# One key projection moved in quarters into the last steps of attention C

## The reference

```python
proj = u @ w_in[l]
qa, ka, va, qb, kb, vb, qc, kc, vc, gl = jnp.split(proj, split_at, axis=-1)
oa = neighbourhood_attention(...)                       # attention A, 8 heads of 64
ob = sliding_window_attention(apply_rope(qb), apply_rope(kb), vb, sw_sink[l])   # B, 8 q heads, 2 k/v heads
oc = differential_attention(apply_rope(qc), apply_rope(kc), vc, ...)            # C, 4 double heads
# inside C: a = softmax(q1 k1) - lam * softmax(q2 k2); o = a @ v; rmsnorm(o, subln_g) over the 128 values of a head
yb = branches @ w_branch[l];  merged = sum(sigmoid(gl + b_gate) * yb);  h = h + rmsnorm(merged @ w_out[l])
```

## Time and profile before

| what | us |
|---|---|
| median of 3 runs | 3376.05 (3374.82 to 3377.39) |
| the profiled execution, its own time | 3378.53 |
| its span, from the first to the last instruction | 3376.7 |
| PE busy | 3318.4 (98% of the span) |
| DVE busy | 2444.0 (72%) |
| ACT busy | 1688.9 (50%) |
| POOL busy | 845.7 (25%) |

### The profile page before, as it was taken

The page is one execution under the profiler, slowest core; times in us unless marked ns, Lnnn a source line. Parts: engine busy times, 40 slices in busy tenths (PEclk is TensorE's granted clock), DMA queues, the critical chain, the costliest instruction groups (busy, mean ns, idle before and its releaser), DMA issues. The chain is left out here.

```text
span 3376.7 us, 51734 instructions
## 1 busy us (share of the span) xinstructions
PE 3318.4 (98%) x20422; PEld 2953.5 (87%) x20422; DVE 2444.0 (72%) x3936; ACT 1688.9 (50%) x3071; POOL 845.7 (25%) x607
## 2 busy tenths in 40 slices
PE   9999999999999999999999999999999999999998
PEld 7999887878889998999887888889988888888998
DVE  7878765756697779777766656697768676649776
ACT  5545453635454445445454544454546374335543
POOL 3433111021054414432111021063400001206431
PEclk9999999999999999999999999999999999999999
DMA  4333433262223332333433253233332222322332
GB/s 138 106 99 114 112 94 86 68 144 91 88 94 104 102 108 75 106 106 114 110 84 94 70 151 99 69 100 103 105 97 92 88 83 69 105 91 92 98 109 82
DMA packets 118049, 332.79 MB, mean 99 GB/s; under 512 B 18984, under 2 KB 21800, under 8 KB 117808
## 3 DMA queue, kind: packets, MB, share of 16 engines
q1 hardware_dynamic: 105200, 306.30, 28.9%
q0 software_dynamic: 12320, 22.66, 3.3%
q10 hardware_dynamic: 288, 0.52, 0.1%
HBM read 306.23 MB, written 4.21 MB: 92 GB/s over the span
## 5 line engine op out<-in xcount | busy, mean ns | idle before, releaser
L1906 DVE TENSOR_TENSOR wl<-raw,wh 128x1024 fp32r<-128x1024 f32 (+2 forms) x633 | 801.2, 1270 | 276.8 <-ACT wh L1328 270.5
L1328 ACT ACTIVATE wh<-raw 128x1024 fp32r<-128x1024 f32 (+2 forms) x637 | 553.5, 875 | 385.1 <-PE PS L807 367.3
L807 PE MATMUL PS<-bh,wh 128*128 128x256 f32 x2520 | 708.5, 281 | 14.6 <-ACT tmp L1328 8.6
L807 PE MATMUL PS<-bl,wh 128*128 128x256 f32 x2520 | 702.7, 279 | 0.0
L807 PE MATMUL PS<-bh,wl 128*128 128x256 f32 x2520 | 702.7, 279 | 0.0
L807 PE MATMUL PS<-uh,wh 128*128 128x512 f32 (+2 forms) x1656 | 615.5, 372 | 13.5 <-DVE ul L1942 6.7
L807 PE MATMUL PS<-uh,wl 128*128 128x512 f32 (+2 forms) x1656 | 602.7, 364 | 0.0
L807 PE MATMUL PS<-ul,wh 128*128 128x512 f32 (+2 forms) x1656 | 602.3, 364 | 0.0
L807 PEld LDWEIGHTS PS<-bh,wh 128*128 128x128 f32 x2520 | 472.9, 188 | 23.1 <-DVE wl L1906 10.8
L807 PEld LDWEIGHTS PS<-bl,wh 128*128 128x128 f32 x2520 | 473.4, 188 | 0.0
L807 PEld LDWEIGHTS PS<-bh,wl 128*128 128x128 f32 x2520 | 471.9, 187 | 0.4
(11 more groups left out here) (268 smaller groups left out, 5748.6 us busy)
## 6 DMA issues: line engine op xcount, KB each, us to landing
raw<-in_gu SPq DMA_DIRECT2D x218, 512.0 KB, 3.3
raw<-in_win SPq DMA_DIRECT2D x139, 512.0 KB, 3.3
raw<-in_dn SPq DMA_DIRECT2D x80, 320.0 KB, 2.9
raw<-in_dn SPq DMA_DIRECT2D x40, 512.0 KB, 3.6
raw<-in_wbr SPq DMA_DIRECT2D x72, 256.0 KB, 2.7
raw<-in_wout SPq DMA_DIRECT2D x24, 512.0 KB, 3.2
raw<-in_dn SPq DMA_DIRECT2D x40, 256.0 KB, 2.6
raw<-in_wv SPq DMA_DIRECT2D x20, 512.0 KB, 3.2
```

Source lines behind the costliest of these rows:

```text
L807: return e.matmul(out, lhs, rhs, start=start, stop=stop, skip_group_check=True)
L1328: return e.activation(out, in_, f, scale=scale, **more)
L1906: tt(wl[:, c % 4, 0:n], src, wh[:, c % 4, 0:n], SUB).then_inc(*S.lo.up(("lo", c)))
```

## The change

The k projection of attention B is no longer a job of its own after attention C. `attention` makes its generator (`tail`) for attention C and takes one piece of six matmuls from it at steps n = 16, 17, 18 and 20. The piece stands ahead of what else the step does. The fourth piece, at n = 20, stands ahead of the sums of the last head. Only PE's program is touched.

```diff
@@ -1134,6 +1134,7 @@
                 A = ATT[st]
                 jobs = iter(fill.jobs)
                 now, left = iter(()), [0]
+                tail = dense(JOBS["k", v, "B", 0], v, "u") if st == "C" else iter(())
...
@@ -1164,6 +1165,8 @@
                             scores(v, st, n, b, qs[hh], *ks[hh], S.sc, (st, v, n))
                     if n < len(fill.quota):
                         filler(fill.quota[n])
+                    elif n in (A.n, A.n + 1, A.n + 2, A.n + 4):
+                        next(tail, None)
...
@@ -1248,7 +1251,6 @@
                 values(v, "C")
                 attention(v, "C", FILLS[v, "C"])
-                run(JOBS["k", v, "B", 0], v)
                 late = [JOBS["q", v, "B", 0], JOBS["t", v, "B"], JOBS["g", v, 1, 0], JOBS["g", v, 1, 1]]
```

## The result

The changed kernel took 3370.05 us (median of 13 runs, 3365.88 to 3374.96) where the kernel before took 3377.24 in the same comparison (13 runs, 3372.07 to 3383.62). The ratio of the times is 0.9982, with a 95% interval from 0.9974 to 0.9989. So by the ratio it is faster by about 6 us, between 3.7 and 8.8; the two medians are 7.2 apart. The forecast was 3369.0, a gain of 7.0.

What follows compares the result with a forecast made beforehand. PE, busy 98% of the span, was taken as the bound. Per mixer -2.75 (waits) - 1.72 (clock) + 0.97 (given back) = -3.50 us, -7.0 for two: 3376.05 - 7.0 = 3369.0 us, range 3364.3 to 3373.3.

Steps and rivals of the forecast that it cites:

- Term 1: Tail of attention C: the quarters of k cover PE's waits and their wake, -2.75 us per mixer.
- Term 2: k projection behind the tail: the granted clock no longer falls, -1.72 us per mixer.
- the clock still falls: Rival, behind the tail: only the waits go, nothing is given back, -5.5 us in all, 3370.5 us; chance 0.13.
- Term 3: Up to the branch products: DVE turns k only behind the diagonals, so +0.97 us per mixer is given back.
- The sum: Terms 1 to 3 together: -3.50 us per mixer, -7.0 for two, 3369.0 us by the median.
- The jam at attention A: Rival, start of attention A: small time shifts make a mixer 4.2 us cheaper or dearer, 3364.8 or 3373.2 us; chance 0.15.
- The slower rival: k's rotation lands late and stops PE at the branch products; at twice its time +3.7, 3379.7 us; chance 0.05.
- more is given back: Rival, tail: more given back or quarters wait; last sums 1.5 us later, gain 2.0 per mixer, 3372.0 us; chance 0.12.

Runs made afterwards that it cites:

- the useless quarter: Kernel before, plus six dense matmuls into k's bank, overwritten afterwards, ahead of the last head's sums: 3373.07 us, ratio 0.9992 [0.9983, 1.0001].

## Why the prediction was right

**Term 1, the waits, -2.75 us per mixer.** Right. The tail with k took 13.09 us where 13.05 was worked out: 10.36 + 5.44 - 13.09 = 2.71 us were gained. Seen from S, the 44.65 of before with the clock and the giveback taken away gives 44.65 - 1.61 - 40.35 = 2.69. All quarters covered their waits, also the fourth, whose margin was thin. That the sum is so near is luck in part: the four quarters took 1.48, 1.48, 1.46 and 1.48 us, 5.90 in all and not 5.44, and the short matmuls 13.09 - 5.90 = 7.19 and not 7.61. The two errors cancel. For the fourth quarter the longer time was of use: it started at 522.36, and the squares of head 3 were ready at 523.14 + 0.59 = 523.73, so that 1.36 us would have been just too short.

**Term 2, the clock, -1.72 us.** The size was right where the clock falls (1.61 by the useless quarter). The reason was only half right. I had taken the fall for an effect of ten light microseconds, and the quarters spread over them as its cure. The runs show that for the fall behind the last sums the last quarter decides: with the three others alone it fell in four of four tails, with the fourth alone in none of two. The one fall inside the tail shows that the last wait is not the only place for it, and why it comes at one place, at the other or not at all stays open. And the term was too large by the share of tails without a fall: over eight tails of before it is 7/8 of 1.6, 1.4 us. The prediction had one profile of before and took the fall, the same in both of its mixers, for fixed. The rival "the clock still falls" did not come true in any of the four tails of the changed kernel.

**Term 3, the giveback, +0.97 us.** Right in its mechanism, a little high: it measured 41.23 - 40.35 = 0.88, 0.56, 0.77 and 0.75 us in four tails. The spread is that of the landing of k's rotation, which now stands in the chain: 5.61, 5.29, 5.49 and 5.48 us from POOL's issue to DVE's release in the same tails. Its chain ran as written: the diagonals ended 528.56 - 523.84 = 4.72 us after the sums' start (4.77 foretold), the first diagonal product had no wait, and the wait for the low parts was 1.14 us where "about 1.2" was foretold. The turning of k ahead of the norms takes it away, which shows that the late turning is its cause.

**The sum.** Mean S over the profiles is 44.46 before and 41.09 now, so 6.7 us for both mixers, beside 7.0 forecast and 6.1 by the ratio of the times. That it is so near is again luck in part: the clock term was 0.3 us per mixer too large, the giveback 0.2 too large, and they have opposite signs. The profiled executions alone differ by 10.8 us in their spans, which is more than the change: 7.2 are the two stretches, 1.6 had come before the first tail, which starts earlier by that much with nothing changed ahead of it, 3.0 came between the two stretches, and 1.1 was lost again behind the second. The 3.0 lie mostly at attention A: in this execution the first mixer of the changed kernel did not lose the clock behind its wait. In its second profile it did. The 60 us of the table by stretches there, before:

```profile
700.00:760.00 60.00, 56.66 (x265) 47.20 (x264) 35.69 (x83) 24.95 (x50) 18.79 (x21) 0.94 0.73 169
```

and in the changed kernel:

```profile
700.00:760.00 60.00, 57.14 (x291) 48.01 (x290) 39.40 (x97) 27.88 (x58) 18.95 (x19) 1.00 0.73 173
```

**The rivals.** The jam at attention A does fall out differently, but from one execution to the next and in every kernel, not by the change: its waits were between 2.4 and 4.0 us in the first mixer of before, over four profiles, and between 1.4 and 2.9 in the second. This is probably part of why executions of one kernel spread over ten microseconds. The slower rival, a late landing of k's rotation, did not come in its size: from issue at 530.04 to DVE's release at 535.65 it took 5.61 us, against 5.33 before. Its mechanism is there in small, in the 0.3 us by which the giveback differs between tails. And "more is given back" did not come.

## What to carry to other kernels

Work moved into waits gains the waits only as far as the engines behind it follow: here DVE went on turning k in its old place, so three of the four quarters brought 0.6 us of the 1.3 they had covered, until DVE's order was changed too. Look for the wait behind which the clock mostly falls: one quarter job in that place was worth about 3 us per mixer, half of it by the clock and half by the work. And where executions of one kernel spread over more than the effect, measure the stretch that the change touches, in several profiles, rather than the span of one.

## What the runs showed of the hardware

The granted clock fell to half behind a wait of only 1.2 us, when short transposes and products stood ahead of it and one-column sums behind it, in 10 of 12 tails. The low clock began 1 to 2 us after the start of the sums, when the dense matmuls of the next job were already running. In one tail it fell earlier, behind waits of 0.74 and 0.36 us, and came back while only products of 128x128 ran. Three quarters of dense matmuls 3 to 11 us ahead of the last sums did not prevent the fall; one right ahead of them went with no fall in any of 16 tails.

At attention A the waits stand behind and ahead of dense matmuls, and there it is a matter of chance too. Of 28 such waits in the fourteen profiles, the seven of 0.7 to 1.7 us were followed by no fall, and of the 21 from 1.9 to 4.0 us 16 were followed by half the clock (or had it already at their end) and five were not. The longest of the five, 2.86 us, is in the changed kernel's first mixer:

```profile
721.12 0.47 PE L807 MATMUL PS<-uh,wh 128*128 128x512 f32 x1 [2.86 <-DVE stkf L2495]
721.43 0.39 PE L807 MATMUL PS<-uh,wl 128*128 128x512 f32 x1
```

A wait of 1.90 us in the kernel with the first three quarters was followed by a fall. The fall is not a fixed property of the program either: the same instructions with the same wait kept the full clock in one tail of eight. So one profile of a clock effect is not enough to price it.
